# A decoder trunk with three branches on one core: rotary score products in pairs of pages, two products on 128 rows, and a table load, a low part and bank waits behind the prompt's heads

## The chip, the core and the metric

One Trainium2 chip, one of its cores. The metric is the device time of one execution in microseconds; three runs of the kernel before gave a median of 1589.9 us (1588.88 to 1589.93).

## What is computed

One inference step of a decoder trunk of two layers, for a prompt of 256 tokens and for 8 sequences of 8 new tokens each with 2048 cached positions (16 pages of 128). What matters here is the attention of the new tokens over the cached pages and over themselves, the causal attention of the prompt, and the spatial-gating branch:

```python
def attend(q_nope, q_pe, k_nope, k_pe, v, mask):
    s = (jnp.einsum('...qhd,...khd->...hqk', q_nope, k_nope)
         + jnp.einsum('...qhr,...kr->...hqk', q_pe, k_pe)).astype(jnp.float32) * ATTN_SCALE
    p = jax.nn.softmax(jnp.where(mask, s, NEG_INF), axis=-1).astype(v.dtype)
    return jnp.einsum('...hqk,...khd->...qhd', p, v)
# mla_sample, for one sequence: the latents of 16 pages and of the new tokens
k_nope, v = expand_kv(lat, w_ukv, k_nope_norm)   # k_nope is normalised per head
return attend(qn, qp, k_nope, kp, v, mask)
# sgu_branch: v in chunks of 128 tokens, w lower triangular
s = jnp.einsum('gts,bcsgd->bctgd', w, vp) + jnp.swapaxes(b_s, 0, 1)[:, :, None]
return u * s, v
```

## The kernel before

Everything is computed for 320 columns (T): 256 prompt tokens and 64 new ones. Each operand of a large product is split into a high part of type fp32r and the rest, a low part, and a product is run three times (high by high, high by low, low by high). The weights come as a stream of units of 128x1024, which ACT (w_hi) and DVE (w_lo) split. The program of each engine is written out by hand, in the order in which it runs, and semaphores tie the engines; nothing is moved by a scheduler. The eight banks of PSUM are handed on by semaphores bank_free, which the engine that reads a bank increments in `release(b)`.

A layer runs `project`, `spatial_and_attention_inputs`, `prompt_attention`, `pages`, `pages_end_and_first_round`, `second_round` and `ffn`, one function of each name per engine.

`prompt_attention` runs eight heads. For a head PE computes scores (`scores`, L984 to L988), DVE takes their maximum (`masked_max`, L1963 to L1966), ACT the exponentials (`exps`), DVE normalises (`normalised`, L1974 to L1977), PE transposes (L1014), ACT copies to pT, and PE multiplies by the values (`values`, L997 and L998) into the banks PAIR_BANK = (4, 6, 7, 5), one for two heads, which ACT (`pair_hi`) and DVE (`pair_lo`) empty. In the middle of the heads PE transposes v to tokens (`v_transposed`, L967) and multiplies by the spatial weights (`spatial`, L976 for 128 rows, L978 for the 64 new tokens), ACT and DVE compute the gate of that branch, y2, and split it. DVE also takes the low part of the spread rotary queries q128 (`rotary_spread_lo`, L1934). At head 6 ACT loads its logarithm and exponential table (`log_and_exp_tables`, L1318).

`pages` runs the 8 sequences, 16 pages each. Two of them are written out, then one more, then a hardware loop over pairs, then the last. The pages are loaded by SP in chunks of two, 4 chunks deep (tpage), with the latent transposed (256 columns) and the rotary key in 128 more: its 32 rows stand there four times, two times as high part and two times as low part, against the high and low parts of the query. ACT takes the high part of a chunk (`pages_hi`), DVE the low part of the latent (`pages_lo`, L1745) and POOL the low half of the rotary rows (`rotary_lo`, L711). For a page PE runs in `keys` one rotary product of 64 columns into bank 4, 5 or 6 and then twelve products of 288 columns into two banks, of which 256 are keys and 32 absorbed scores:

```python
r0 = HT * (p % (NPG // 2))
mm(PS[:, rotary_bank(p, par), r0:r0 + HT], lt_hi[:, t, i, 256:384], q128_of(b), start=True, stop=True)
```

ACT squares the keys (ksqp) and copies the scores (sraw), DVE sums the squares per head (kss, L2097). A sequence later its scores are finished: DVE multiplies them by the norms and adds the rotary scores from PSUM (`finished_scores`, at pages 4 and 5), takes the maximum over pages (`halves_max`, `page_max` L2051), PE transposes it (`seq_max`, L1058), DVE takes the row maximum, and PE spreads it over all rows with a product of 64 rows (`seq_spread`, L1063), DVE subtracts (`shift`), and ACT takes the exponential. Two sequences later the values of the pages are added (`page_values`, L1081 and L1082, at most two products a page), with rows loaded by SP (rrow), split by ACT (r_hi) and POOL (r_lo, L739). Before `pages` PE waits for seven banks and for q128; DVE splits y2 into y2_lo and copies snew before sequence 0, and POOL, before it goes on in sequence 0, waits for y2_lo and copies ones into r_hi (L753), since that lies over what y2_lo is computed from.

## Time and profile before

| | |
|---|---|
| median of 3 runs | 1589.9 us |
| profiled execution, its own time | 1589.27 us |
| its span in the trace | 1587.4 us |
| granted clock of TensorE | full in all slices |
| stages of pages | about 140 to 393 us and 927 to 1181 us |

The profile is of one execution. Its span runs from the first to the last instruction; the execution's own time has 1.9 us around it. Engines: PE is TensorE's products, PEld its weight loads, DVE VectorE, ACT ScalarE, POOL GpSimd, SP the queue that issues transfers. A PE row's duration holds the latency of its pipeline, so the rate of PE is read from one start to the next. The two layers run alike; times are quoted from the first.

### The profile page before, as it was taken

To read this page: it belongs to the slowest core of one execution; us is meant where nothing else is said; L and a number is where in the kernel's file an instruction comes from. 1 tells how busy PE (TensorE), PEld (TensorE's weight loads), DVE (VectorE), ACT (ScalarE), POOL (GpSimd) and SP (SyncE) were. 2 spreads that over 40 slices of the span, in tenths; PEclk is the share of its full clock that TensorE was granted. 3 is DMA by queue.
4 is the path that set the end of the run, shared out by engine and by line. 5 is a ranking of instruction groups with operands and counts; after the bars stand their busy time and mean duration, and the time that the engine had idled before them with its cause. 6 is when DMAs were issued, how large, how long until landed. Compare 5 with 4: busy or idle time off the path is not lost.

```text
span 1587.4 us, 33215 instructions
## 1 busy us (share of the span) xinstructions
PE 1561.0 (98%) x10860; PEld 1516.9 (96%) x10860; DVE 1068.7 (67%) x1626; ACT 884.6 (56%) x1612; POOL 521.1 (33%) x659
## 2 busy tenths in 40 slices
PE   7999999999999999999999999999999999999999
PEld 7987999999999999999999789999999999999999
DVE  6787777777664766664376877777775748666633
ACT  5786676767534444443357866666764345444432
POOL 3732377776700000000058213767667001000000
PEclk9999999999999999999999999999999999999999
DMA  7331455553544444444454224655535444444443
GB/s 274 120 108 52 139 183 167 163 161 109 186 134 155 151 147 146 150 155 146 146 188 136 76 73 137 196 152 166 163 111 174 145 154 151 147 146 146 151 152 112
DMA packets 114690, 232.90 MB, mean 147 GB/s; under 512 B 12881, under 2 KB 78706, under 8 KB 114450
## 3 DMA queue, kind: packets, MB, share of 16 engines
q1 hardware_dynamic: 112178, 223.13, 45.3%
q0 software_dynamic: 2400, 8.36, 1.6%
q8 instruction: 60, 0.98, 0.3%
q14 instruction: 52, 0.43, 0.1%
HBM read 228.98 MB, written 2.46 MB: 146 GB/s over the span
## 4 chain that ended last, share of the span: by engine, by line
PE 90%; DVE 4%; ACT 2%; DVEq 1%; issue 1%; ACTq 1%; DMA 0%; POOL 0%; SPq 0%; POOLq 0%
PE PS L803 53%; PE PS L1048 26%; PE PS L1081 2%; PE PS L1082 2%; DVE w_lo L1742 1%; PE PS L1043 1%; ACT w_hi L1297 1%; DVEq L1736 1%; PE PS L830 1%; PE PS L859 1%; ACTq L1301 0%; ACT r_hi L1297 0%; PE PS L937 0%; ACTq L1485 0%; DMA x<-in_xT 0%
## 5 line engine op out<-in xcount | busy, mean ns | idle before, releaser
L1742 DVE TENSOR_TENSOR w_lo<-raw,w_hi 128x1024 fp32r<-128x1024 f32 x258 | 325.0, 1261 | 222.9 <-ACT w_hi L1297 220.0
L1297 ACT ACTIVATE w_hi<-raw 128x1024 fp32r<-128x1024 f32 x258 | 272.3, 1057 | 347.3 <-PE PS L803 333.1
L803 PE MATMUL PS<-h_hi,w_hi 128*128 128x320 f32 x1360 | 426.4, 314 | 11.1 <-DVE h_lo L1769 10.3
L803 PE MATMUL PS<-h_hi,w_lo 128*128 128x320 f32 x1360 | 421.3, 310 | 0.0
L803 PE MATMUL PS<-h_lo,w_hi 128*128 128x320 f32 x1360 | 421.3, 310 | 0.0
L803 PEld LDWEIGHTS PS<-h_hi,w_hi 128*128 128x128 f32 x1360 | 256.3, 188 | 14.2 <-issue 9.5
L803 PEld LDWEIGHTS PS<-h_lo,w_hi 128*128 128x128 f32 x1360 | 256.4, 189 | 0.9
L803 PEld LDWEIGHTS PS<-h_hi,w_lo 128*128 128x128 f32 x1360 | 256.2, 188 | 0.0
L1048 PE MATMUL PS<-comb_hi,lt_hi 128*128 128x288 f32 x1024 | 239.9, 315 | 0.0
L1297 ACT ACTIVATE ksqp<-PS 128x512 f32<-128x512 f32 x256 | 153.2, 598 | 152.4 <-PE PS L1048 150.3
L2097 DVE TENSOR_REDUCE kss<-ksqp 128x8 f32<-128x512 f32 x256 | 174.2, 682 | 85.3 <-ACT ksqp L1297 84.2
L1048 PE MATMUL PS<-comb_hi,lt_lo 128*128 128x288 f32 x1024 | 218.7, 295 | 0.0
L1048 PE MATMUL PS<-comb_lo,lt_hi 128*128 128x288 f32 x1024 | 218.6, 294 | 0.0
L739 POOL TENSOR_TENSOR r_lo<-rrow,r_hi 128x512 fp32r<-128x512 f32 x128 | 167.7, 1314 | 42.1 <-issue 23.0
L711 POOL TENSOR_TENSOR lt_hi<-tpage,lt_hi 64x256 fp32r<-64x256 f32 x128 | 118.5, 925 | 169.7 <-ACT lt_hi L1297 165.3
L1048 PEld LDWEIGHTS PS<-comb_lo,lt_hi 128*128 128x128 f32 x1024 | 164.0, 188 | 0.0
L1048 PEld LDWEIGHTS PS<-comb_hi,lt_lo 128*128 128x128 f32 x1024 | 163.9, 188 | 0.0
L1048 PEld LDWEIGHTS PS<-comb_hi,lt_hi 128*128 128x128 f32 x1024 | 158.9, 189 | 0.0
L1745 DVE TENSOR_TENSOR lt_lo<-tpage,lt_hi 128x512 fp32r<-128x512 f32 x128 | 109.5, 856 | 26.9 <-ACT lt_hi L1297 26.6
L803 PE MATMUL PS<-hid_hi,w_lo 128*128 (+1 forms) x352 | 108.8, 309 | 0.0
L803 PE MATMUL PS<-hid_lo,w_hi 128*128 (+1 forms) x352 | 108.8, 309 | 0.0
L803 PE MATMUL PS<-hid_hi,w_hi 128*128 (+1 forms) x352 | 108.8, 309 | 0.0
(317 smaller groups left out, 2662.0 us busy)
## 6 DMA issues: line engine op xcount, KB each, us to landing
raw<-in_stream SPq DMA_DIRECT2D x258, 512.0 KB, 3.5
tpage<-in_tcache SPq DMA_DIRECT2D x256, 192.0 KB, 2.4
rrow<-in_rcache SPq DMA_DIRECT2D x256, 128.0 KB, 2.6
x<-in_xT SPq DMA_DIRECT2D x2, 640.0 KB, 6.9
sbias<-in_sbias POOLq DMA_DIRECT2D x2, 640.0 KB, 6.2
out_yT<-x SPq DMA_DIRECT2D x4, 320.0 KB, 2.2
const<-in_consts SPq DMA_DIRECT2D x1, 1088.0 KB
wgate<-in_wgate POOLq DMA_DIRECT2D x2, 512.0 KB, 4.5
```

The costliest lines, as they stand in the source:

```text
L711: nc.gpsimd.tensor_tensor(half, tpage[64:128, c % TBUF, :, 256:384], f(half), ALU.subtract).then_inc(pt_rope.sem, 1)
L739: nc.gpsimd.tensor_tensor(r_lo[:, at, :], rrow[:, src, :], f(r_hi[:, at, 0:KVL]), ALU.subtract).then_inc(rows_split.sem, 1)
L803: done = mm(out, w[:, slot, c], a, start=first and n == 0 and m == 0, stop=last and n == len(pairs) - 1 and m == 2)
L830: last = mm(out, lhsT, r, start=n == 0, stop=n == len(rhss) - 1)
L859: mm(PS[:, b, 0:T], wgate[:, g, j, :], xc[:, j, :], start=True, stop=True).then_inc(lgate_mm.sem, 1)
L1048: last = mm(PS[:, 2 * s + g, c0:c0 + 288], a[:, t, i, 128 * k:128 * k + 128], w[:, k, g, c0:c0 + 288], start=k == 0 and n == 0, stop=k == ...
L1081: mm(PS[:, 7, 0:KVL], w, r_lo[:, r, :], start=False, stop=False)
L1082: last = mm(PS[:, 7, 0:ROW], w, r_hi[:, r, :], start=False, stop=p == NPG - 1)
L1297: return nc.scalar.activation(out, in_, func, **kw)
L1742: V.tensor_tensor(w_lo[:, s, :], raw[:, s, :], f(w_hi[:, s, :]), ALU.subtract).then_inc(lo_done.sem, 1)
L1745: return V.tensor_tensor(out, whole, f(hi_), ALU.subtract)
L2097: V.tensor_reduce(kss[:, par, p, :], ksqp[:, s, :].rearrange("p (h c) -> p h c", h=H), AX.X, ALU.add).then_inc(pk_ss.sem, 1)
```

## The change

Four things are changed.

**Rotary scores.** The cache's rotary keys are laid out in blocks of 64 positions: the two halves of a page stand one above the other in 64 rows, high and low part make 128, and a chunk has 2 x 64 columns of them. PE runs one product of 256 columns for a chunk, in its second page: q_rot holds the high and the low part of the query, each for both halves with zeros between. The two results lie 128 elements apart in bank 6 or 5, and DVE adds them into srot with one reduction a chunk. POOL writes q_rot in `queries`. The key products keep their shapes, but take the same half of the two pages of a chunk together, and rrow is loaded in the same order. `finished_scores` adds srot instead of reading PSUM, and the waits on s_rot go away.

**128 rows.** `seq_spread` multiplies all 128 rows of mx, of which POOL zeroes the lower 64 once a layer. The new tokens' v is transposed together with 64 prompt tokens, and wss has 128 rows with zeros.

**Order in the heads.** ACT copies v_tokens before it squares ua. DVE has no rotary_spread_lo. ACT's table load moves from head 6 to page 10 of sequence 0.

**Behind the heads.** DVE's y2_lo moves to page 2, its copy of snew to page 6 of sequence 0. PE waits for banks 0 to 3 before sequence 0, for banks 6 and 5 at their first rotary products, and for 4 and 7 after the sequence.

```diff
@@ load_tpages, load_rows
-                sp.dma_start(rrow[:, (2 * m + i) % RRAW, :],
-                             ins["rcache"][bass.ds(l * NPHYS + at[i], 1)].rearrange("o p n -> p (o n)")
+                sp.dma_start(rrow[64 * i:64 * i + 64, 2 * m % RRAW:2 * m % RRAW + 2, :],
+                             ins["rcache"][bass.ds(l * NPHYS + at[i], 1)].rearrange("o (v r) n -> (o r) v n", v=2)
@@ POOL, queries
+                nc.gpsimd.tensor_tensor(hi_, both, half, ALU.mult)
                 pool.drain()
...
+                nc.gpsimd.tensor_tensor(lo_, both, f(hi_), ALU.subtract)
+                pool.drain()
+                nc.gpsimd.tensor_tensor(lo_, f(lo_), half, ALU.mult).then_inc(qc.sem, 1)
@@ POOL, sequence
                         for i in range(RROWS):
                             nc.gpsimd.tensor_copy(r_hi[:, i, KVL:ROW], ones[:, 0:2])
+                        pool.drain()
+                        nc.gpsimd.memset(mx[HT:128], 0.0)
                         pool.drain().then_inc(p_free.sem, 1)
@@ PE
-                mm(PS[:, 4 + g, SEQ:T], v_tokens[0:TS, 2, 128 * g:128 * g + 128], wss[:, g, :], start=True, stop=True).then_inc(sgu_mm.sem, 1)
+                mm(PS[:, 4 + g, SEQ:T], v_tokens[:, 2, 128 * g:128 * g + 128], wss[:, g, :], start=True, stop=True).then_inc(sgu_mm.sem, 1)
...
+        def rotary_scores(l, b, c, par):
+
+            pe.wait_ge(pt_rope.sem, pt_rope.at(l, b * NCH + (c + 1)))
+            if isinstance(b, int) and b == 0 and c < 2:
+                pe.wait_ge(bank_free[6 - c].sem, banks.last(l, 6 - c))
+            else:
+                pe.wait_ge(rot_added.sem, rot_added.at(l, b * NCH + (c - 1)))
+            mm(PS[:, 6 - c % 2, 0:4 * HT], lt_hi[:, c % 2, 4], q_rot[:, par].rearrange("p s c -> p (s c)"),
+               start=True, stop=True)
...
-            if p == NPG // 2 and not (isinstance(b, int) and b == 0):
-                pe.wait_ge(s_rot.sem, s_rot.at(l, b * 2))
-            r0 = HT * (p % (NPG // 2))
-            mm(PS[:, rotary_bank(p, par), r0:r0 + HT], lt_hi[:, t, i, 256:384], q128_of(b), start=True, stop=True)
+            if i == 1:
+                rotary_scores(l, b, p // CHUNK, par)
...
-            mm(PS[:, 4 + par, 128:128 + HT], ones[0:HT, :], mx[:, 1:1 + HT], start=True, stop=True).then_inc(s_mb.sem, 1)
+            mm(PS[:, bank, 128:128 + HT], ones[:], mx[:, 1:1 + HT], start=True, stop=True).then_inc(s_mb.sem, 1)
...
-            for b in (0, 1, 2, 3, 4, 6, 7):
+            for b in range(4):
+                pe.wait_ge(bank_free[b].sem, banks.last(l, b))
+            sequence(l, 0, 0, tail=False, values=False, older=False)
+            for b in (4, 7):
@@ ACT
             exps(0)
-            A(ge[:], ua[:], ACT.Square).then_inc(gsq.sem, 1)
             v_copied(l, 0, 4)
             v_copied(l, 1, 5)
             v_copied(l, 2, 7)
+            A(ge[:], ua[:], ACT.Square).then_inc(gsq.sem, 1)
...
-                if h == 6:
-                    log_and_exp_tables()
...
+                if not tail and p == 10:
+                    log_and_exp_tables()
@@ DVE
-            rotary_spread_lo(l, 0)
-            rotary_spread_lo(l, 1)
-            release(6)
...
+        def rotary_scores(l, b, c, par):
+
+            V.tensor_reduce(srot[:, par, 2 * c:2 * c + 2].rearrange("p v c -> p (v c)"),
+                            PS[:, 6 - c % 2, 0:4 * HT].rearrange("p (s x) -> p x s", s=2), AX.X, ALU.add).then_inc(rot_added.sem, 1)
...
+                if not tail and p == 2:
+                    dve.wait_ge(y2h.sem, y2h.at(l, 1))
+                    lo(y2_lo[:], ge[:], y2_hi[:]).then_inc(y2_ready.sem, 1)
+                if not tail and p == 6:
+                    dve.wait_ge(sn_ready.sem, sn_ready.at(l, 1))
+                    V.tensor_copy(snew[TS:2 * TS], snew[0:TS]).then_inc(sn_ready.sem, 1)
```

On PE, at the start of the stage of pages, there stood before (comb and lt are the key products' operands, q the spread query):

```order
L997 MATMUL PS<-pT,vp 64x256
L998 MATMUL PS<-pT,vp 64x128
L1043 MATMUL PS<-q,lt_hi 128x64
L1048 MATMUL PS<-comb_hi,lt_hi 128x288 x2
L1048 MATMUL PS<-comb_lo,lt_hi 128x288 x2
L1048 MATMUL PS<-comb_hi,lt_lo 128x288 x2
```

and the same place of the change, with the numbers at the rows' start since its rows read alike (the keys' rows of page 0 are 572 to 577, those of page 1 follow row 578):

```order
571 L1011 MATMUL PS<-pT,vp 64x128
572 L1064 MATMUL PS<-comb_hi,lt_hi 128x288 x2
573 L1064 MATMUL PS<-comb_lo,lt_hi 128x288 x2
574 L1064 MATMUL PS<-comb_hi,lt_lo 128x288 x2
575 L1064 MATMUL PS<-comb_hi,lt_hi 128x288 x2
576 L1064 MATMUL PS<-comb_lo,lt_hi 128x288 x2
577 L1064 MATMUL PS<-comb_hi,lt_lo 128x288 x2
578 L1043 MATMUL PS<-q_rot,lt_hi 128x256
```

The rotary product stands ahead of every second page now, and has 256 columns.

On DVE, at the same place, before (y_lo from PS is a pair of heads, y_lo from ge is y2_lo):

```order
L1745 TENSOR_TENSOR y_lo<-PS,y_hi 128x256 x3
L1745 TENSOR_TENSOR lt_lo<-tpage,lt_hi 128x512
L1745 TENSOR_TENSOR y_lo<-ge,y_hi 128x1280
L2017 COPY snew<-snew 64x512
L2097 TENSOR_REDUCE kss<-ksqp 128x8 x2
```

and in the change:

```order
L1757 TENSOR_TENSOR lt_lo<-tpage,lt_hi 128x512
L1757 TENSOR_TENSOR y_lo<-PS,y_hi 128x256 x2
L2098 TENSOR_REDUCE kss<-ksqp 128x8 x2
L2040 TENSOR_REDUCE srot<-PS 128x128
L1757 TENSOR_TENSOR lt_lo<-tpage,lt_hi 128x512
L2098 TENSOR_REDUCE kss<-ksqp 128x8
L1757 TENSOR_TENSOR y_lo<-ge,y_hi 128x1280
```

y2_lo has moved behind the sums of three pages, and the first reduction of rotary scores stands among them.

On POOL, around the start of sequence 0, the change has (lt_hi is the low half of the rotary rows):

```order
L722 TENSOR_TENSOR lt_hi<-tpage,lt_hi 64x128 x2
L764 CAST r_hi<-ones 128x2 x4
L766 MEMSET mx 64x67
L722 TENSOR_TENSOR lt_hi<-tpage,lt_hi 64x128 x14
```

The four copies, which wait for y2_lo, stand between the low halves of chunks 1 and 2, as before; the zeroing is new, and the low halves have 64x128 for 64x256.

## Rows read from the trace of the kernel before

**Rows 1.** The page's table of engines: busy us, share of the span, instructions

```profile
PE 1561.0 (98%) x10860; PEld 1516.9 (96%) x10860; DVE 1068.7 (67%) x1626; ACT 884.6 (56%) x1612; POOL 521.1 (33%) x659
```

**Rows 2.** Timeline of PE, sequence 0: start us, us, engine, line, operation

```profile
142.26 0.19 PE L1043 MATMUL PS<-q,lt_hi 128*128 128x64 f32 x1
...
142.64 0.42 PE L1048 MATMUL PS<-comb_lo,lt_hi 128*128 128x288 f32 x2
142.90 0.43 PE L1048 MATMUL PS<-comb_hi,lt_lo 128*128 128x288 f32 x2
...
143.96 0.19 PE L1043 MATMUL PS<-q,lt_hi 128*128 128x64 f32 x1
```

**Rows 3.** DVE in one sequence of the loop: stretch, us, busy, clock, DMA

```profile
259.68:292.34 32.66, 24.84 (x42) 1.00 0.54 163
```

**Rows 4.** Timeline of PE, a sequence of the loop, pages 13 to 14

```profile
322.54 0.28 PE L1081 MATMUL PS<-r_lo,p_hl 128*128 128x256 f32 x1
322.65 0.28 PE L1082 MATMUL PS<-r_hi,p_hl 128*128 128x258 f32 x1
...
322.86 0.43 PE L1063 MATMUL PS<-mx,ones 64*128 64x64 f32 x2
...
323.23 0.30 PE L1043 MATMUL PS<-q,lt_hi 128*128 x1
```

**Rows 5.** Timeline of PE, transposes of va and spatial products

```profile
111.93 1.47 PE L967 MATMUL PS<-const,va 128*128 128x128 f32 x12
...
116.23 0.71 PE L976 MATMUL PS<-wsp,v_tokens 128*128 128x128 f32 x4
116.88 0.43 PE L978 MATMUL PS<-wss,v_tokens 64*128 64x64 f32 x2
117.24 0.71 PE L976 MATMUL PS<-wsp,v_tokens 128*128 128x128 f32 x4
```

**Rows 6.** Timeline of all engines, heads to first page: [idle before <-releaser]

```profile
123.84 0.29 DVE L1963 TENSOR_REDUCE pst<-PS 128x1 f32<-128x128 f32 x1 [1.04 <-PE PS L988]
...
136.17 1.28 ACT L1318 ACT_TABLE_LOAD   x1 [0.16 <-issue]
...
136.91 0.55 PE L1014 MATMUL PS<-const,sp_ 128*128 128x128 f32 x3 [1.23 <-DVE sp_ L1977]
...
138.89 0.65 PE L997 MATMUL PS<-pT,vp 128*64 128x256 f32 x2
...
140.60 0.51 PE L1048 MATMUL PS<-comb_hi,lt_hi 128*128 128x288 f32 x2
```

**Rows 7.** Groups by line and shape: busy us, mean ns, idle before

```profile
L1297 ACT ACTIVATE ksqp<-PS 128x512 f32<-128x512 f32 x256 | 153.2, 598 | 152.4 <-PE PS L1048 150.3
L2097 DVE TENSOR_REDUCE kss<-ksqp 128x8 f32<-128x512 f32 x256 | 174.2, 682 | 85.3 <-ACT ksqp L1297 84.2
...
L2051 DVE TENSOR_REDUCE m<-mxh 128x64 f32<-128x512 f32 x16 | 17.3, 1084 | 1.4
...
L1964 DVE TENSOR_REDUCE pst<-PS 128x1 f32<-128x256 f32 x16 | 6.6, 413 | 0.0
```

**Rows 8.** Line L1745: duration ns min/median/max, first and last start

```profile
L1745 DVE TENSOR_TENSOR y_lo<-ti,y_hi x2: 1483/1483/1483, 106.8 to 893.9; 128x1280 fp32r<-128x1280 f32 x2
```

**Rows 9.** Timeline of POOL, sequence 0

```profile
143.75 0.70 POOL L753 CAST r_hi<-ones 128x2 fp32r<-128x2 f32 x4 [1.52 <-DVE y_lo L1745]
145.85 1.07 POOL L711 TENSOR_TENSOR lt_hi<-tpage,lt_hi 64x256 fp32r<-64x256 f32 x1 [1.41 <-ACT lt_hi L1297]
```

**Rows 10.** Groups by line and shape, POOL

```profile
L698 POOL TENSOR_TENSOR comb_lo<-qabs,comb_hi 128x64 fp32r<-128x64 f32 x32 | 9.9, 330 | 2.4 <-issue 0.8
```

**Rows 11.** Timelines of PE and DVE, sequence 1, pages 7 and 8

```profile
179.62 0.20 PE L1043 MATMUL PS<-q,lt_hi 128*128 128x64 f32 x1
...
180.97 0.68 DVE L1745 TENSOR_TENSOR lt_lo<-tpage,lt_hi 128x512 fp32r<-128x512 f32 x1
...
181.71 0.30 PE L1043 MATMUL PS<-q,lt_hi 128*128 128x64 f32 x1 [0.23 <-DVE lt_lo L1745]
```

More of the change, by code:

```diff
@@ L1926, in spatial_and_attention_inputs @@
             lo(y0_lo[:], ti[:], y0_hi[:]).then_inc(y0_ready.sem, 1)
-        def rotary_spread_lo(l, jt):
-            dve.wait_ge(q128_hi.sem, q128_hi.at(l, 1))
-            for r in (1, 3):
-                rows = slice(32 * r, 32 * r + 32)
-                dst = q128[rows, :, 32 * jt:32 * jt + 32].rearrange("p b (h t) -> p h b t", h=4)
-                src = PS[rows, 6, :].rearrange("p (h j b t) -> p h j b t", h=4, j=2, b=NB)[:, :, jt]
-                last = V.tensor_tensor(dst, src, f(dst), ALU.subtract)
-            last.then_inc(q128_ready.sem, 1)
         def new_latent_lo(l):
@@ L2010, in prompt_attention @@
             normalised(7)
-            for j in range(1, 4):
-                pair_lo(l, j)
+            pair_lo(l, 1)
             pages_lo(l, 0, 1)
-            dve.wait_ge(y2h.sem, y2h.at(l, 1))
-            lo(y2_lo[:], ge[:], y2_hi[:]).then_inc(y2_ready.sem, 1)
-            dve.wait_ge(sn_ready.sem, sn_ready.at(l, 1))
-            V.tensor_copy(snew[TS:2 * TS], snew[0:TS]).then_inc(sn_ready.sem, 1)
+            pair_lo(l, 2)
+            pair_lo(l, 3)
         def pair_lo(l, j):
@@ L2032, in finished_scores @@
             half = NPG // 2
-            at, bank = (slice(half, NPG), 6) if second else (slice(0, half), 4 + par)
+            at = slice(half, NPG) if second else slice(0, half)
             inv = kss[:, par, at].rearrange("p a (h o) -> p a h o", o=1).to_broadcast([128, half, H, NT])
@@ L2037, in finished_scores @@
             dve.drain()
-            into = sraw[:, par, at].rearrange("p a c -> p (a c)")
-            last = V.tensor_tensor(into, into, PS[:, bank, :], ALU.add)
-            last.then_inc(s_rot.sem, 1)
+            V.tensor_tensor(sraw[:, par, at], sraw[:, par, at], srot[:, par, at], ALU.add)
+        def rotary_scores(l, b, c, par):
+            V.tensor_reduce(srot[:, par, 2 * c:2 * c + 2].rearrange("p v c -> p (v c)"),
+                            PS[:, 6 - c % 2, 0:4 * HT].rearrange("p (s x) -> p x s", s=2), AX.X, ALU.add).then_inc(rot_added.sem, 1)
         def of_seq(t, b):
```

131 lines of the change are left out of this document (67 added, 64 removed).

## Prediction

> **What bounds the kernel now.** I read the page's table of engines first, then the timeline of TensorE over the cache pages, then the rows of the engine that TensorE waits for at each place where its rhythm breaks. The table shows PE busy 98% of the span and DVE 67% [rows 1]: almost everything that shortens the time must shorten PE's own row, or one of its few waits. The clock was granted in full throughout. In sequence 0 a page is one rotary product and twelve key products, and pages start every 1.70 us (142.26 to 143.96, [rows 2]). Where I say page 8 or page 12 I mean the place in a sequence of 16 pages. The loop over the later sequences is the same rhythm with two value products more per page. DVE is busy 24.8 of 32.7 us in a sequence of the loop [rows 3], so 8 us are free there, but in pieces.
>
> **The rotary products.** A pair of key products starts every 0.265 us (12 products are 1.59 us), so of the 1.70 us the one 64-column rotary product costs 0.106 us [rows 2]. The change runs one product of 256 columns per two pages instead of two of 64. The nearest row is a value product with 256 columns, after which the next starts 0.11 us later [rows 4]; I take 0.12. A chunk of two pages saves 2 x 0.106 - 0.12 = 0.09 us, 64 chunks a layer: **5.9 us a layer**. The bounds are narrow, 5.5 to 6.5.
>
> **The spread of the maximum.** It has 64 rows now. From the last value product (322.65 + 0.12) to the next page at 323.23 pass 0.46 us for two passes of 64 columns [rows 4]. With 128 rows the nearest price is the transposes of va, 12 in 1.47 us with their tail, 0.12 each [rows 5]: two are 0.24. Saving 0.22 x 8 = **1.8 us a layer** (bounds 0 and 2.7). The zeroing of mx is one small POOL instruction a layer.
>
> **The new tokens' spatial products.** A group of four passes with 128 rows takes 0.65 us (116.23 to 116.88), and the two with 64 rows 0.36 (to 117.24) [rows 5]. At 0.12 each the six would take 0.72 instead of 1.01: 1.2 us over four groups. Besides, the square of ua is behind the three copies of v_tokens now, so that PE need not wait for the third. The third transpose has 128 columns for 64: under 0.2 us. DVE loses four subtractions (rotary_spread_lo). PE comes out about 1.5 us sooner, and the heads can use it, since DVE stood 1.04 us for PE's scores in the middle of them [rows 6]. I take **1.5 us a layer**, between 0.4 (ACT's row is then the bound) and 2.4.
>
> **The table load and the bank waits.** The load of 1.28 us at 136.17 stands on ACT between the last head's exponentials and the next copy of pT. The last head's transposes end at 136.91 + 0.55 = 137.46; a copy of 0.5 and a semaphore later its value product could start at 138.1; it starts at 138.89. From there PE needs some 0.7 us (the product's row is 0.65), and the first page could start at 138.8. It starts at 140.60, because it waits for seven banks, whose last is released by DVE [rows 6]. Now it waits for banks 0 to 3 only: **1.8 us a layer** (bounds 0.8 and 2.0). In its new place, page 10 of sequence 0, the load lies in ACT's idle time; if that cover were gone it would cost its 1.28 us.
>
> **What is late next: y2's low part.** This is the one new wait that I price against the change. DVE splits y2 after page 2 of sequence 0 now. POOL waits for it before it copies ones into r_hi, and behind that wait stands POOL's low half for chunk 2, for which PE's rotary product in page 5 waits. Counted from the first key product: pages 0 to 2 end at 3 x 1.59 + 0.12 = 4.9; ACT's square 0.60 and DVE's reduction 0.68 with two semaphores make 6.3 [rows 7]; the split takes 1.48 with POOL idle [rows 8]: 7.8. POOL then takes 0.17 and 0.70 for the four copies, some 0.3 for the zeroing and two drains, 0.25 to its next instruction and some 0.45 for it (64x128 now, between the 0.33 of a 128x64 and the 1.07 of a 64x256) [rows 9, 10]: 9.7 to 9.9. PE reaches the product at 5 x 1.59 + 2 x 0.12 = 8.2. **PE stands some 1.6 us a layer** (0 to 2.5). The start of y2's high part and SP's loads of rows come later too, but nothing needs them before sequence 2.
>
> **The reductions on DVE.** DVE gets one reduction a chunk: 256 PSUM elements, summed in pairs 128 elements apart. The trace has no such read. Its bounds are the 256 contiguous PSUM elements at 413 ns, and the per-element rate of the strided SBUF row. The contiguous rows of 512 and 256 elements (682 and 413 ns) give 1.05 ns an element and 144 ns a start; the strided one has (1084 - 144)/512 = 1.84 ns, which for 256 and a start gives 0.62 us [rows 7]. I take 0.50, 0.45 in the row of a busy engine. Eight are 3.6 us a sequence, so DVE comes to 28.5 of 32. Where DVE is slack that is hidden. It is not at page 8: in sequence 1 PE's page 8 starts 2.09 us after page 7 instead of 1.71, at 181.71, and the wait ends with DVE's lt_lo, started 180.97 [rows 11]. The reduction of page 5 lies on that chain, and PE's three pages before it are 0.15 shorter: it costs 0.6 there. A second place is page 12, behind page_max: 0.4 more by the same reckoning. That gives back 1.0 us in sequence 1. In the loop the same chain has 3 x 0.24 us more room, so of the 0.38 + 0.6 some 0.3 are left a sequence, six times 1.8. **Together 2.8 us a layer** (0 to 5).
>
> The Trainium skill says on its page Vector Engine (DVE) Microarchitecture Reference, section Measured stream behaviour on trn2, that an SBUF port keeps its rate only for runs of at least two adjacent words, and that a source hopping every element takes 1.73 instead of 1.05 ns. By that rule the reduction would take about 0.59 us (an estimate from that page) and the sum would come out some 2 us higher. The strided row of this trace (1.84 ns) agrees with it for SBUF in kind; that page gives no figure for PSUM, and no row here has one.
>
> **Other parts.** ACT's high copy of pages has 640 for 768 elements, and POOL's low half is half as long, both off the path. POOL's queries get three 128x128 operations a sequence, some 1.4 us, against the eight shorter halves. The last add of scores reads SBUF for PSUM. They cost nothing while POOL keeps a microsecond of lead into the next sequence; if not, the first pages wait some tenths.
>
> **Sum.** A layer saves 5.9 + 1.8 + 1.5 + 1.8 = 11.0 and gives back 1.6 + 2.8 = 4.4: 6.6, for two layers 13 us. The profiled execution took 1589.27 us beside a span of 1587.4, and becomes 1576.3; the median of the three runs lies 0.6 above it: **1577 us** (0.8% faster; its own range 1572 to 1582).
>
> **Rivals.**
> Nothing is given back: y2's split comes early enough or POOL catches up, and DVE's idle pieces take the reductions. For it: DVE has 8 us free a sequence. Against it: the wait at page 8 is there already. 2 x 11.0 off: 1568.
> DVE is the bound in places: the reduction takes its upper bound, and heads gain only 0.7 because ACT's row sets their pace. Then 1.5 us a layer more go in the stages of pages and 0.8 in the heads, and POOL's longer queries hold up some first pages: 1583.
> The gain at the heads is only a deferral: DVE enters sequence 0 later by the y2 split and the copy of snew, and all that PE won is spent in waits there, while the loop is held by DVE at today's pace. 1588 to 1590.
> Slower: DVE becomes the bound everywhere. It decides from (32 - 25)/8 = 0.85 us a reduction; if pairs from PSUM cost what the whole strided row costs now, 1.08 us [rows 7], DVE needs 24.8 + 8.6 + 0.6 = 34.0 us a sequence instead of 32.7, some 9 us a layer over seven sequences, against which the heads and sequence 0 save 2.4 in all: 6.6 a layer, 1603. For it speaks only that PSUM's price is unseen; against it that the row has twice the elements.
>
> **Chances.** Forecast 0.48, nothing given back 0.17, DVE in places 0.18, deferral 0.10, slower 0.07. A measurement of this kernel can tell 0.2% (3.2 us) from no change. The first three are faster (0.83), the deferral is no change (0.10), the last slower (0.07). The range has to take in 1568 and 1583 with an edge for unknown prices: 1566 to 1587.
>
> **What would show it.** PE's pages in the middle of sequence 0 should start 1.59 and 1.71 us apart by turns; the 256-column rotary product should cost its successor 0.12 us. A wait of PE at page 5 of sequence 0 should end with POOL's low half, about 1.6 us long. The first key product should come 3.3 us sooner after the layer's start. The reduction's duration decides most of the rest: at 0.41 the loop's sequence should be 31.6 us, at 0.62 over 32.2. If the first key product comes no sooner, the heads' terms are wrong; if the loop's sequences stay at 32.7, those of the rotary products are.

## The result, and the profile after

The changed kernel takes **1595.33 us** (median of 6 runs, 1594.70 to 1596.18) where the kernel before, on the same chip, takes 1589.91 (6 runs, 1588.88 to 1590.93): 5.4 us longer, ratio 1.0035 with the interval [1.0022, 1.0048]. The forecast was 1577, its range 1566 to 1587. The profiled execution took 1595.93 us beside a span of 1594.1.

The page's table of engines, after (answers to [rows 1]):

```profile
span 1594.1 us, 33203 instructions
PE 1547.3 (97%) x10732; PEld 1502.8 (94%) x10732; DVE 1117.2 (70%) x1746; ACT 870.6 (55%) x1612; POOL 519.6 (33%) x709
```

PE has 13.7 us less to do and DVE 48.5 more. So PE does not work longer, it waits longer. What it waits for, in the waits of PE after (what it waited for, us in total, times, longest):

```profile
PE PS L1064 <- DVE lt_lo L1757: 18.3, 24, 1.7
PE PS L1094 <- POOL r_lo L750: 4.0, 10, 1.2
PE PS L1043 <- ACT sraw L1309: 2.8, 2, 1.4
```

The first row is new in its size: before, a page began with its rotary product, and those products waited 0.4 us in all for lt_lo. The third is the wait at page 5 of sequence 0. The gain and the loss by stage, from the timelines of PE, for layer 1 and layer 2 (a layer's heads are counted from the first product with wv_first to the first key product, a sequence from its first key product to that of the next):

| stage | before | after | difference |
|---|---|---|---|
| heads | 38.8, 38.4 | 36.5, 36.2 | -2.3, -2.2 |
| sequence 0 | 27.1, 27.1 | 28.0, 28.0 | +0.9, +0.9 |
| sequence 1 | 28.7, 28.7 | 28.8, 28.8 | 0.0, 0.0 |
| sequence 2 to the last value product | 244.0, 244.9 | 248.7, 248.6 | +4.7, +3.7 |
| ahead of layer 1's heads, and from layer 1's last value product to layer 2's heads | 101.9, 448.5 | 101.1, 450.1 | -0.8, +1.6 |

The differences sum to the 6.7 us between the spans. The last line holds nothing that the change touches; its parts differed by 1 to 2 us between other profiles of this study too, and its +1.6 is a matter of TensorE's clock: from 804.9 to 808.2 us of the profile after it was granted at half (1.2 for 2.4 GHz), behind three waits of PE of 0.4 us each; the profile before has it in full there. The loss lies in the loop: a sequence there takes 33.8 to 34.1 us (in layer 2 every second one 32.9) against some 32.8 before [rows 3]. The rest of the two profiles is told where the stall is.

PE at page 8 of a loop sequence, after (start, length, engine, line, what; in brackets the idle time before it and its releaser): it stands for 1.73 us.

```profile
276.05 0.28 PE L1095 MATMUL PS<-r_hi,p_hl 128*128 128x258 f32 x1
278.06 0.53 PE L1064 MATMUL PS<-comb_hi,lt_hi 128*128 128x288 f32 x2 [1.73 <-DVE lt_lo L1757]
```

What DVE did up to there, and POOL beside it, after (same columns):

```profile
270.85 0.69 DVE L2098 TENSOR_REDUCE kss<-ksqp 128x8 f32<-128x512 f32 x1 [0.22 <-ACT ksqp L1309]
271.45 0.95 DVE L2034 TENSOR_TENSOR sraw<-sraw,kss 128x512 f32<-128x512 f32 x1
272.48 1.53 DVE L2036 TENSOR_TENSOR sraw<-sraw,srot 128x512 f32<-128x512 f32 x1
273.92 0.67 DVE L2098 TENSOR_REDUCE kss<-ksqp 128x8 f32<-128x512 f32 x1
274.52 0.41 DVE L2040 TENSOR_REDUCE srot<-PS 128x128 f32<-128x256 f32 x1
274.85 0.67 DVE L2034 TENSOR_TENSOR sraw<-sraw,kss 128x512 f32<-128x512 f32 x1
275.60 1.52 DVE L2036 TENSOR_TENSOR sraw<-sraw,srot 128x512 f32<-128x512 f32 x1
277.05 0.88 DVE L1757 TENSOR_TENSOR lt_lo<-tpage,lt_hi 128x512 fp32r<-128x512 f32 x1
...
272.17 1.29 POOL L750 TENSOR_TENSOR r_lo<-rrow,r_hi 128x512 fp32r<-128x512 f32 x1 [0.32 <-issue]
...
275.04 1.53 POOL L750 TENSOR_TENSOR r_lo<-rrow,r_hi 128x512 fp32r<-128x512 f32 x1 [0.32 <-issue]
```

The same piece of the kernel before, DVE and then POOL, in rows that the prediction did not read:

```profile
272.30 0.69 DVE L2097 TENSOR_REDUCE kss<-ksqp 128x8 f32<-128x512 f32 x1 [0.47 <-ACT ksqp L1297]
272.90 0.96 DVE L2036 TENSOR_TENSOR sraw<-sraw,kss 128x512 f32<-128x512 f32 x1
273.94 0.69 DVE L2039 TENSOR_TENSOR sraw<-sraw,PS 128x512 f32<-128x512 f32 x1
...
275.90 0.69 DVE L2039 TENSOR_TENSOR sraw<-sraw,PS 128x512 f32<-128x512 f32 x1
276.50 0.68 DVE L1745 TENSOR_TENSOR lt_lo<-tpage,lt_hi 128x512 fp32r<-128x512 f32 x1
...
273.63 1.29 POOL L739 TENSOR_TENSOR r_lo<-rrow,r_hi 128x512 fp32r<-128x512 f32 x1 [0.32 <-issue]
```

From the start of the reduction of page 4 to the end of lt_lo DVE took 4.88 us before (272.30 to 277.18) and 7.08 after (270.85 to 277.93). The 2.20 us more are the two adds (2 x 0.83 = 1.67), the new reduction (0.33, to the start of the next instruction) and lt_lo (0.20). The add is as large as before; what has changed is that its second operand is srot in SBUF where it was PSUM, and that it runs beside a subtraction of POOL with two SBUF operands. Beside the same POOL instruction the add from PSUM took 0.69.

Not every add of the change is stretched. In the two sequences of layer 2's loop that take 32.9 us both adds take 0.8, and POOL's subtraction starts 0.6 us after them where it starts 0.3 to 0.6 before them elsewhere; page 8 then starts 2.4 us after page 7, for 3.7 in the other sequences of the loop. So one execution of one kernel shows both cases, 1.0 us a sequence apart. In all, 14 of the 32 adds took 1.5 us.

The groups of DVE over a loop sequence (stretch 258 to 292, count, busy us, mean ns), after:

```profile
L2040 DVE TENSOR_REDUCE srot<-PS 128x128 f32<-128x256 f32 x9 | 3.7, 412 | 0.0
L2036 DVE TENSOR_TENSOR sraw<-sraw,srot 128x512 f32<-128x512 f32 x2 | 3.0, 1524 | 0.1
```

The reduction takes 0.41, the lower of its two bounds (0.41 and 0.62, taken at 0.50). The row that the prediction valued at nothing, the add, is the dear one.

From here on, **theory A**: page 8 waits for the two halves of the finished scores that stand in a row on DVE, and these grew by the stretched adds. **Theory B**: DVE is short of time as a whole, from 128 reductions.

### The profile page after: what moved, and what is told of

The parts are those of the page before. It is cut to its first block, busy times and chain, and to the rows that moved or that the text cites. A ratio compares the mean times of both kernels' runs of the same rounds, so it can differ in the third digit from the quotient of the medians.

```text
span 1594.1 us, 33203 instructions
## 1 busy us (share of the span) xinstructions
PE 1547.3 (97%) x10732; PEld 1502.8 (94%) x10732; DVE 1117.2 (70%) x1746; ACT 870.6 (55%) x1612; POOL 519.6 (33%) x709
## 4 chain that ended last, share of the span: by engine, by line
PE 76%; DVE 11%; DVEq 4%; ACT 3%; issue 3%; ACTq 1%; DMA 1%; SPq 0%; POOL 0%; POOLq 0%
PE PS L816 53%; PE PS L1064 17%; DVEq L2035 2%; DVE lt_lo L1757 2%; DVE kss L2098 2%; DVE w_lo L1754 1%; PE PS L1094 1%; ACT ksqp L1309 1%; PE PS L1095 1%; DVEq L1748 1%; ACT w_hi L1309 1%; DVE m L2052 1%; DVE srot L2040 1%; DVE sraw L2036 1%; PE PS L1043 1%
## 5 line engine op out<-in xcount | busy, mean ns | idle before, releaser
L1064 PE MATMUL PS<-comb_hi,lt_hi 128*128 128x288 f32 x1024 | 224.4, 300 | 19.1 <-DVE lt_lo L1757 18.3
L2098 DVE TENSOR_REDUCE kss<-ksqp 128x8 f32<-128x512 f32 x256 | 170.9, 679 | 61.1 <-ACT ksqp L1309 60.2
L722 POOL TENSOR_TENSOR lt_hi<-tpage,lt_hi 64x128 fp32r<-64x128 f32 x128 | 80.3, 628 | 165.9 <-ACT lt_hi L1309 157.4
```

The lines of the kernel that those rows point to most:

```text
L722: nc.gpsimd.tensor_tensor(half, tpage[64:128, c % TBUF, :, 4], f(half), ALU.subtract).then_inc(pt_rope.sem, 1)
L1064: last = mm(PS[:, 2 * s + g, c0:c0 + 288], a[:, t, 2 * k + i], w[:, k, g, c0:c0 + 288], start=k == 0 and n == 0, stop=k == 1 and n == 2)
L2098: V.tensor_reduce(kss[:, par, p, :], ksqp[:, s, :].rearrange("p (h c) -> p h c", h=H), AX.X, ALU.add).then_inc(pk_ss.sem, 1)
```

## The experiments

Each was timed beside the kernel before; the ratio is to that, and it is what compares kernels of different rounds best. Line numbers of rows are those of the kernel that the rows are from; edits are to the changed kernel where nothing else is said.

**1. Without the add.**

```diff
-            dve.drain()
-            V.tensor_tensor(sraw[:, par, at], sraw[:, par, at], srot[:, par, at], ALU.add)
```

> The add of the rotary scores to the key scores is left out (two instructions of 512 elements a sequence on DVE, line 2036), with its drain. The output leaves the rotary part of the sample scores out. THEORY A, the chain to page 8: the wait of PE for DVE's low half at page 8 is ended by the two halves of finished scores that stand in a row on DVE at pages 4 and 5; the adds take 1.52 us each there, where before they took 0.69. Without them the chain is 3.0 us shorter, the loop's sequence falls from 33.9 to 31.9 or 32.2 us, and the kernel takes 1570 to 1578. THEORY B, sheer load: DVE is filled by the 128 reductions; the add is 3 of its 29.4 us a sequence, and the time falls by no more than the load is above some limit: 1585 or more.

Measured: 1578.40 us, ratio 0.9932 [0.9918, 0.9945]: 17 us less than the changed kernel for 32 instructions of 1.11 us on average. The loop's sequences take 32.1 to 32.9 us. PE's wait for lt_lo is down to 5.2 us from 18.3:

```profile
PE PS L1064 <- DVE lt_lo L1757: 5.2, 13, 0.5
```

Just above A's range, and far from B's. But it takes the whole add away, its old 0.69 us too.

**2. Short reductions.**

```diff
-            V.tensor_reduce(srot[:, par, 2 * c:2 * c + 2]...,
+            n = 2 * HT if isinstance(b, int) and b < 2 else 8
+            V.tensor_reduce(srot[:, par, 2 * c:2 * c + 2]...[:, 0:n],
```

> From sequence 2 on the reduction over two products sums 8 of 128 columns, so that it takes some 0.16 us for 0.41; the order and every wait stay. The output leaves out most of the rotary part there. THEORY A (chain to page 8): of the eight reductions a sequence only the one of page 5 (and that of page 7, for pages later) lies on the chain, so a loop's sequence of 33.9 us gains 0.25 to 0.6, and the kernel takes 1588 to 1593. THEORY B (sheer load of the reductions): 2.0 us less DVE work in each of six sequences of two layers gives most of it back, 1.5 or more a sequence: 1577 or less.

Measured: 1594.07 us, ratio 1.0027 [1.0018, 1.0036], 1.3 us less than the changed kernel, which the two intervals do not tell apart from nothing. Page 8 starts 3.45 us after page 7 instead of 3.70: the saving of the one reduction of page 5, and hardly anything for the seven others. In layer 2 all the loop's adds are stretched now, and the two sequences that took 32.9 us take 33.5, which uses up part of the gain. B falls. A's range (1588 to 1593) was missed by a microsecond.

**3. The pieces apart.**

```diff
-                if tail and p in (4, 5):
-                    finished_scores(l, b - 1, 1 - par, p == 5)
+                if tail and p in (4, 6):
+                    finished_scores(l, b - 1, 1 - par, p == 6)
-                if tail and p == 7:
+                if tail and p == 8:
                     halves_max(l, b - 1, 1 - par)
-                if tail and p == 9:
+                if tail and p == 10:
                     page_max(l, b - 1, 1 - par)
```

> Same work, same instructions: the second half of the finished scores stands after page 6 instead of page 5, halves_max after 8 instead of 7, page_max after 10 instead of 9, so that the low half of the next pages stands between the two long pieces. THEORY A (chain to page 8): no piece between two low halves is longer than 2.5 us, PE's waits at pages 8 and 12 mostly go, the loop's sequence falls from 33.9 to 32.0 to 32.6 and the kernel takes 1572 to 1582. THEORY B (sheer load): DVE has the same 29.4 us a sequence to do; the kernel takes 1593 to 1597.

Measured: 1591.95 us, ratio 1.0012 [1.0003, 1.0021], a miss for A's number and for B's. The wait at page 8 is gone in every sequence (1.6 to 1.8 us for up to 3.7), but PE now stands in page 11, before the transpose of the maxima (L1071), for up to 1.7 us, since page_max comes after it is wanted:

```profile
PE PS L1071 <- issue: 10.2, 8, 1.5
PE PS L1071 <- DVE m L2054: 8.7, 6, 1.7
```

The same profile has the add in both conditions, within one sequence. The first starts while POOL's r_lo runs, the second while a copy of POOL (L734) does. DVE, then POOL:

```profile
272.78 1.53 DVE L2036 TENSOR_TENSOR sraw<-sraw,srot 128x512 f32<-128x512 f32 x1
...
277.51 0.73 DVE L2036 TENSOR_TENSOR sraw<-sraw,srot 128x512 f32<-128x512 f32 x1
...
272.47 1.28 POOL L750 TENSOR_TENSOR r_lo<-rrow,r_hi 128x512 fp32r<-128x512 f32 x1 [0.32 <-issue]
...
276.83 0.86 POOL L734 CAST p_hl<-prob 128x256 fp32r<-128x256 f32 x1
277.83 1.01 POOL L736 TENSOR_TENSOR p_hl<-prob,p_hl 128x256 fp32r<-128x256 f32 x1
```

The add takes 0.73 us where POOL's copy has only 0.18 us left to run, and 1.53 where r_lo has 0.97 left (272.78 to 273.75). Both adds end 0.55 us after the POOL instruction that was running when they started (273.75 to 274.31, 277.69 to 278.24), as if the add waited for its end. That holds for every such add of this study: in each of the nine profiles with all adds from SBUF, 26 of the 32 started beside a running POOL instruction, and all of them end 0.54 or 0.55 us after it; those that started alone take 0.69.

**4. The change without its rotary products.** From the kernel before: table load at page 10, the square behind the copies, 128-row products, y2's low part after page 2, bank waits behind the heads.

> The kernel before, with every part of the change but the paired rotary products: table load at page 10, the square of ua behind the copies, spatial and spread products on 128 rows, y2's low part after page 2, bank waits behind the heads. The low part of q_rot stays with DVE in the heads. THEORY A: the head's gain (2.1 to 2.3 us a layer) and the spread's (0.22 x 8) are real and y2's low part costs 1.6 us at page 4 or 5 of sequence 0: 2.4 us a layer less than before, 1583 to 1587. RIVAL, deferral: what the head gains is waited for in sequence 0, and the spread's gain is lost to DVE's chain: 1589 to 1591.

Measured: 1592.56 us, ratio 1.0017 [1.0008, 1.0026], slower than before and outside both ranges. The heads save 2.3 and 1.7 us and the spread 0.32 a sequence (page 14 after 2.17 us for 2.49), but sequence 0 takes 33.7 us (32.6 in layer 2) for 27.1: its rotary product stands in page 4, a page sooner than the paired one, and needs POOL's low half of chunk 2 there:

```profile
141.61 0.19 PE L1048 MATMUL PS<-q,lt_hi 128*128 128x64 f32 x1
147.19 0.39 PE L1048 MATMUL PS<-q,lt_hi 128*128 128x64 f32 x1 [3.73 <-issue]
150.43 0.26 PE L1048 MATMUL PS<-q,lt_hi 128*128 128x64 f32 x1
```

Page 5 starts 3.1 us after it, for 1.7, and that is the clock: during the stand of 3.73 us it fell, and it was granted at half up to 152.4. By the starts of the pages behind the stand that cost 2.4 us in layer 1 and 1.4 in layer 2. A stretch of page 4 (us, busy of PE, PEld, DVE, ACT and POOL, then the granted clock, 0.50, and DMA):

```profile
147.20:150.30 3.10, 3.10 (x13) 3.10 (x14) 0.00 (x0) 0.00 (x0) 0.72 (x1) 0.50 0.42 128
```

With the old rotary products y2's move is dearer.

**5. An add from PSUM, first try.**

```diff
+                    pe.wait_ge(pt_lo.sem, pt_lo.at(l, b * NCH + 5))
                     seq_sums(l, b - 3, 4)
...
-            V.tensor_tensor(sraw[:, par, at], sraw[:, par, at], srot[:, par, at], ALU.add)
+            V.tensor_tensor(into, into, PS[:, 4, :], ALU.add)
```

> The changed kernel with one operand replaced: the two adds of a sequence read 512 columns of PSUM (bank 4) where they read srot in SBUF; the reductions stay, and so does all else (PE waits at page 6 for the low half of chunk 4 before the sums, which it does at page 8 anyway). The sample scores have no rotary part. THEORY A (both DVE and POOL fetch two SBUF operands, and slow each other): the add is back at 0.69 us in the loop from 1.52, page 8 stalls 1.6 us less, a loop's sequence takes 32.2 to 32.8 us for 33.9 and the kernel 1579 to 1586, close to the kernel without the add plus 2 x 0.69 us where DVE has no room. THEORY B (the add is long for its own sake, or the load of the reductions is the cause): the add stays over 1.1 us or the sequence over 33.4, and the kernel at 1592 or more.

Measured: 1622.48 us, ratio 1.0200 [1.0186, 1.0214]. The experiment is spoiled by its own wait, which I took for one that PE has anyway; at page 6 it comes two pages early, and behind the long waits the granted clock fell, to 0.987 to 0.992 on average in its runs:

```profile
PE PS L1101 <- DVE lt_lo L1758: 28.2, 10, 3.0
```

What it shows is the duration alone: 0.69 us for every add of the loop.

**6. As 4, with POOL's wait for y2 later.**

```diff
-                    if c == 0 and isinstance(b, int) and b == 0:
+                    if c == 4 and isinstance(b, int) and b == 0:
                         pool.wait_ge(y2_ready.sem, y2_ready.at(l, 1))
```

> As the kernel with the old rotary products and the rest of the change, but POOL's wait for y2's low part (with its four copies of ones and the zeroing) stands after chunk 4 of sequence 0 and not before the low half of chunk 2. THEORY A (that wait is what sequence 0 pays, 5.4 us a layer with a rotary product in page 4): sequence 0 is back at 26.9 us and the kernel takes 1580 to 1584, 6 to 10 less than before. RIVAL (PE's gain in the heads is waited for anyway, since DVE's chain of sums behind y2_lo is what holds page 4): 1589 to 1593.

Measured: 1581.33 us, ratio 0.9941 [0.9927, 0.9954]. Sequence 0 is back at 27.2 us in both layers. POOL's wait, in front of a low half that PE needs at once, is what sequence 0 paid: 11.9 us in the two layers, of which some 4 are the clock behind it.

**7. Finished scores after 4 and 6 only**, halves_max and page_max left at 7 and 9, and the edit of 6.

> The changed kernel with the finished scores after pages 4 and 6 (for 4 and 5), halves_max and page_max where they were (7 and 9), and POOL's wait for y2 after chunk 4 of sequence 0. THEORY A: sequence 0 loses its 1.7 us stall; page 8 does not stall, PE waits at pages 10 to 12 for some 0.5 us; loop's sequence 32.0 to 32.6; kernel 1576 to 1583. THEORY B (any place of these pieces gives the same, since DVE is short of time as a whole): 1588 to 1592, only the stall of sequence 0 gone.

Measured: 1581.53 us, ratio 0.9942 [0.9929, 0.9956], in A's range. Page 8 has no wait; most loop sequences have one at page 10, again for lt_lo (page 10 starts 3.7 us after page 9, for 2.2), and last 33.0 to 33.4 us (two of layer 2's without it 32.2 and 32.6).

**8. Everything behind page_max a page later** (finished scores after 4 and 6, halves_max 8, page_max 10, transpose and row maximum 12, spread and shift 14, exponentials 15), and the edit of 6.

> Finished scores after 4 and 6, halves_max after 8, page_max after 10, and what follows it one page later each: PE's transpose of the maxima at page 12 and its spread at 14, DVE's row maximum at 12 and shift at 14, ACT's exponentials at 15; POOL's wait for y2 after chunk 4 of sequence 0. THEORY A: the 1.7 us that PE stood before the transpose at page 11 are covered too; loop's sequence 31.2 to 32.0; kernel 1569 to 1577. RIVAL: the exponentials come a page later, and POOL's split and PE's first value product at page 3 of the next sequence wait for them: 0.5 to 1.5 us a sequence, 1578 to 1588. THEORY B (DVE is short of time as a whole): 1588 to 1592.

Measured: 1588.04 us, ratio 0.9982 [0.9973, 0.9991]: the upper end of the rival's range, and the lower end of B's. The trace decides between them: no wait is left at pages 8 to 13, but page 0 starts 2.4 to 2.6 us after page 15, for 1.8, and the end of the stage, where the last two sequences have only value products, waits for POOL's r_lo, which comes after the exponentials. At those last waits the granted clock fell to half, for 6.8 us in each layer, which makes up to 7 us in this profile.

```profile
PE PS L1094 <- POOL r_lo L750: 10.1, 12, 3.7
```

**9. The order that fits.** Finished scores after 4 and 6, halves_max after 8, page_max after 10, the transpose of the maxima after 12, and the rest where it was; the row maximum goes ahead of page 12's reduction; and the edit of 6. It computes all that the reference does.

```diff
-                if tail and p == 11:
+                if tail and p == 12:
                     seq_max(l, b - 1, 4)
...
+                if tail and p == 12:
+                    row_max(l, b - 1, 4)
                 dve.wait_ge(pk_sq.sem, pk_sq.at(l, b * NPG + (p + 1)))
```

> The changed kernel with finished scores after pages 4 and 6, halves_max after 8, page_max after 10, PE's transpose of the maxima after page 12 (for 11), DVE's row maximum ahead of the reduction of page 12, and everything behind it (spread, shift, exponentials) where it was; POOL's wait for y2 after chunk 4 of sequence 0. THEORY A (page 8 and page 12 are single places where a piece of DVE work stands ahead of what PE needs): none of the stalls of the earlier orders is left, a loop's sequence takes 31.2 to 31.9 us, and the kernel 1560 to 1570. THEORY B (DVE's load, 29 us in 32, makes a stall come back at another page whatever the order): 32.3 or more a sequence, 1577 or more.

Measured: **1567.57 us** (1566.48 to 1569.70), ratio 0.9863 [0.9848, 0.9878]: 22.4 us under the kernel before, 27.8 under the changed one. The same instructions on DVE, the adds as stretched as in 7 (1130 ns on average in both loops, for 1340 in the changed kernel's: the order takes the second add away from r_lo too), the same reductions. Loop sequences take 31.5 to 32.2 us; one is the distance of these rows of PE (the first value product of a sequence):

```profile
260.65 0.28 PE L1090 MATMUL PS<-r_hi,p_hl 128*128 128x258 f32 x1
...
292.57 0.28 PE L1090 MATMUL PS<-r_hi,p_hl 128*128 128x258 f32 x1
```

The waits of PE have no lt_lo among their large ones any more; what the maxima still cost is this:

```profile
PE PS L1076 <- DVE mx L2060: 1.6, 6, 0.3
```

**10. The changed kernel with the edit of 6 alone.**

> The changed kernel with one edit: POOL's wait for y2's low part, its copies of ones and the zeroing stand after chunk 4 of sequence 0. If the stall in page 5 of sequence 0 comes from that wait, sequence 0 falls from 28.0 to 26.3 us, and the kernel from 1595.3 to 1591.5 to 1592.5. If DVE's split of y2 itself (kss of pages 3 and 4 stand behind it) holds page 5, the stall stays: 1594 to 1596.

Measured: 1591.93 us, ratio 1.0014 [1.0005, 1.0023]: 3.4 us less than the changed kernel, and 24.4 more than 9, which is what the order alone is worth. Its rotary products of sequence 0 start 3.28 us apart throughout, where the changed kernel's go like this:

```profile
139.23 0.28 PE L1043 MATMUL PS<-q_rot,lt_hi 128*128 128x256 f32 x1
142.51 0.28 PE L1043 MATMUL PS<-q_rot,lt_hi 128*128 128x256 f32 x1
147.37 0.36 PE L1043 MATMUL PS<-q_rot,lt_hi 128*128 128x256 f32 x1 [1.42 <-ACT sraw L1309]
```

4.86 for 3.28: 1.58 us lost. The profile names ACT, whose copy came last by its records; POOL's low half was the one that counted, since the edit touches only POOL.

**11. The table load back at head 6.**

> The changed kernel with the load of the table back at head 6. If the load stood between the last head's exponentials and the next copy of pT on the path, the first key product comes 0.6 to 1.3 us later after the layer's first product than in the changed kernel (36.5 us), and the kernel takes 1.2 to 2.6 us longer: 1596.5 to 1598. If the bank waits had hidden it: 1594.5 to 1596.

Measured: 1597.74 us, ratio 1.0044 [1.0030, 1.0057]: 2.4 us more than the changed kernel, with intervals that overlap. The first key product comes 38.0 and 37.1 us after the layer's first product with wv_first (36.5 and 36.2). In layer 1 part of that is the clock, at half from about 137 to 140 us in this profile; layer 2, without it, says 0.9 us for the load. And the wait of the kernel before is back:

```profile
PE PS L1010 <- ACT pT L1309: 1.3, 2, 0.6
```

**12. The order of 9 with the old rotary products.**

> The fastest order so far (finished scores after 4 and 6, halves_max after 8, page_max after 10, transpose of the maxima after 12, POOL's wait for y2 after chunk 4) with the rotary products of the kernel before: one of 64 columns a page, no reductions, adds from PSUM. If the paired products are worth what was forecast (0.09 us a chunk, 64 chunks a layer, 11.8 us in all) where DVE makes nobody wait, this kernel takes 11 to 13 us more than the paired one of the same order: 1578 to 1581. If DVE's reductions and adds still give part of it back there, the gap is smaller: 1570 to 1577.

Measured: 1592.13 us, ratio 1.0009 [1.0000, 1.0017], outside what I expected, and 10.8 us slower than 6, which has the old order. The rotary product of page 8 writes the bank from which the second add reads, and waits for that add, now a page later:

```profile
PE PS L1048 <- DVE sraw L2041: 6.1, 8, 1.3
```

(In six more sequences the profile names ACT's copy for the wait at this place, 3.6 us in all. In the one I read, that copy ended 0.16 us after the add; which of the two counted is not shown.)

So the paired kernel can be ordered in a way that the old one cannot: its rotary scores leave PSUM in two pages. For the worth of the paired products I compare each with the order that suits it: 1567.57 against 1581.33, 13.8 us by the medians, 12.4 by the ratios, 11.8 in the two profiles from the first key product to the last value product of both layers. What of this is PE's own row and what the order cannot be told from these two.

**13 and 14. An add from PSUM, with a control.** In both, the older sequence's sums and normalising stand after page 8 and its transposes and their copy after 10, so that PE touches bank 4 only behind a wait that it has; in 14 the adds read PSUM as in 5.

> A control for the next: the changed kernel with the older sequence's sums after page 8 (for 6), its normalising after 8 (for 7), its transposes after 10 and their copy after 10 (for 9). DVE gets the same work; the pieces in front of page 8 stay: 1594 to 1597, page 8 at 3.5 us or more in the loop.

> The same with the two adds of a sequence reading 512 columns of PSUM (bank 4) for srot in SBUF; PE touches that bank only from page 8 on, behind a wait that it has anyway. The sample scores have no rotary part. THEORY A (the stretch of an add with two SBUF operands beside POOL's is what page 8 waits for): the add takes 0.69 for 1.52 us, page 8 comes 1.6 us sooner and a loop's sequence 1.2 to 1.6: 10 to 16 us under the control. RIVAL (the reduction of page 5 and the adds' bare 0.69 are enough for the stall): under 5 us below the control.

Measured: the control 1613.78 us, ratio 1.0149 [1.0135, 1.0163], the other 1601.90, ratio 1.0072 [1.0060, 1.0084]. The control missed its range by 17 us: the copy of the transposes after page 10 holds up the transpose of the maxima at page 11, a wait that both have (13.4 and 13.2 us, 10 times). Between the two lie **11.9 us**, within A's 10 to 16, but not all by A's way: page 8 starts 3.1 us after page 7 instead of 3.9, 0.8 sooner where A said 1.6. Two things make up the 11.9. PE waits 7.5 us less for lt_lo:

```profile
PE PS L1064 <- DVE lt_lo L1757: 18.1, 16, 2.0
PE PS L1064 <- DVE lt_lo L1757: 10.6, 16, 1.1
```

(control, then the other). The rest is mostly the clock: after PE had stood 1.96 us at page 8, the control's clock was granted at half, and page 9 came 3.4 us after page 8 without a wait in it:

```profile
281.50:284.80 3.30, 3.30 (x17) 3.30 (x16) 3.21 (x5) 0.71 (x2) 1.38 (x2) 0.50 0.42 122
```

The control's runs have a mean granted clock of 0.995 to 0.997, the other's 0.999 to 1.000; 0.003 of 1614 us are some 5 us (an estimate). The changed kernel's profile has the clock in full through both stages of pages, so its own loss there holds nothing of the kind. Where the stretch went shows on DVE (then POOL) of the kernel with the PSUM operand:

```profile
272.43 0.69 DVE L2038 TENSOR_TENSOR sraw<-sraw,PS 128x512 f32<-128x512 f32 x1
...
275.32 1.70 DVE L1757 TENSOR_TENSOR lt_lo<-tpage,lt_hi 128x512 fp32r<-128x512 f32 x1
...
272.12 1.29 POOL L750 TENSOR_TENSOR r_lo<-rrow,r_hi 128x512 fp32r<-128x512 f32 x1 [0.32 <-issue]
...
275.28 1.19 POOL L750 TENSOR_TENSOR r_lo<-rrow,r_hi 128x512 fp32r<-128x512 f32 x1 [0.32 <-issue]
```

The add from PSUM is untouched by POOL's r_lo that started 0.31 us before it; lt_lo, with two SBUF operands, now meets the next one and takes 1.70. (lt_lo, too, ends 0.55 us after r_lo.) Some of what the add no longer pays, lt_lo pays, so that 7.5 us is the price of the stretch in this order, not of the operand in every one.

## Why the prediction was wrong

**The step that failed** stands under "Other parts": "The last add of scores reads SBUF for PSUM. They cost nothing". The add went from 0.69 to 1.53 us in 7 of the 16 sequences, two a sequence, and to 0.8 in five more. It stood on the chain to page 8, which the same prediction had named as the place where DVE has no room [rows 11]; the reduction was priced there and the add was not. Experiments 13 and 14 put its stretch at some 7.5 us of waiting, which agrees with the 1.0 us by which the stretched sequences of layer 2 are longer than the others, seven times; experiment 1 puts the whole add at 17.

How far that goes in the 18 us of the miss: by the prediction's terms, sequence 2 to the last value product should have saved 4.0 us a layer (six times the sum of 0.74 and 0.22, less 1.8), and lost 4.7 and 3.7. These 16 us are most of the miss, and the heads make 2 of the rest; sequences 0 and 1 came out as forecast. About half of the 16 is the stretch. The rest is what else grew on DVE's way to pages 8 and 12, so that the term "0.3 are left a sequence" was too small by more than the add alone: the reduction of page 5 (0.33 us) and lt_lo's own stretch (0.20) stand there, and with adds from PSUM PE still waited 10.6 us for lt_lo. How that rest divides is not shown.

**Two SBUF operands beside POOL.** The rows say that a DVE subtraction or addition with two SBUF operands takes 0.7 us alone and up to 1.7 beside POOL's. The Trainium skill, page SBUF — State Buffer, section Who interferes with whom, says that a DVE instruction with two SBUF inputs contends with a GpSimd instruction that reads SBUF, since its second input comes through the shared read interface. It calls the shared ports an exclusive lock; that whoever issues first has them for the whole instruction it says of DVE's two-port modes. The rows agree, with the whole-instruction part for these instructions too: every add that starts beside a running POOL instruction ends 0.55 us after it, 0.73 or 1.53 us long in experiment 3, and with the PSUM operand it takes 0.69 beside the same POOL row in experiment 14. The kernel before had the sign of it too: lt_lo took 0.68 at 276.50 and 1.23 at 280.32, ending 0.55 us after a subtraction of POOL (279.90 to 281.00).

**The sign of the result** was not in the rival that had it. "DVE becomes the bound everywhere" wanted a reduction of 0.85 us; it takes 0.41, and DVE was no bound: the order of experiment 9 has the same work and runs a sequence in 31.5 to 32.2 us. The stall was local.

**Rotary products: right.** Two pages and one rotary product take 3.28 us in sequence 0, for 3.39: 0.11 saved a chunk, against a forecast of 0.09. In the best order tried for each, the kernels with and without pairing are 12 to 14 us apart, against 11.8. The prediction's sign, that the rotary terms are wrong if the loop's sequences stay at 32.7, would have misled: the sequences grew, and the terms held.

**Spread of the maximum: right, undersized.** Forecast 0.22 us, 0.32 in experiment 4.

**Heads: two thirds.** Forecast 1.5 + 1.8 = 3.3 us a layer, measured 2.3 and 2.2. The table load and the bank waits gave their 1.8: from the last head's transposes to the first key product pass 1.92 us (135.62 to 137.54) for 3.69 [rows 6], and experiment 11 gives the load alone 0.9 of it. The groups of spatial products start 0.67 us apart for 1.00, as forecast, but of the 1.5 us only 0.5 arrived at the first page: PE now waits 1.08 us for DVE (at 120.03) before the first head's value product, where it had no wait before, and the last heads still wait 1.23 us for sp_. The lower bound of 0.4 was near, and its reason (another engine sets the heads' pace) the right one.

**y2's low part: right.** Forecast 1.6 us a layer, 1.58 in the timeline, 3.4 for both layers in experiment 10.

**Reductions: overpriced.** Taken at 0.50 us, with 2.8 us a layer given back. They take 0.41, and experiment 2, which cut them by some 0.25 us each in six sequences of eight, gave 1.3 us in all. The 0.59 us that the prediction worked out from the Trainium skill's figure for a source that hops every element did not come: the measurement decides for 0.41. Besides, the same section excepts a one-source instruction whose stream alternates between two regions and writes one word for two read, as this reduction does (there the regions lay 16 KiB apart, here 512 bytes, in PSUM). The wait at page 8 was named rightly, its cause only in part.

**The forecast gain itself** was there: experiment 9 takes 1567.57, where "nothing is given back" said 1568. That agreement is partly luck, since its order also removes waits of the kernel before (page 8 and 12 of sequence 1) while the heads gave less.

## What to carry to other kernels

When an edit moves an operand from PSUM to SBUF, price the instruction anew: look whether the other vector engine reads SBUF at the same time, and whether somebody waits behind it. A place that is named as having no room must be summed over all that stands there, moved and changed instructions as well as new ones. Before giving up a change that lost time, put its long pieces between the short ones that others wait for: here the order alone was worth 24 us, and each wait had to be followed to its next place (page 8, page 10, page 11, the stage's end) until one order had hardly any. And read the granted clock before you give a difference to one cause: in experiments 4, 5, 8, 11 and 13 it had fallen at a wait of PE, and part of the time was that.

## What was not expected of the hardware

A DVE add of 512 elements with both operands in SBUF took 0.69 us alone; started while an instruction of POOL ran, it ended 0.55 us after that instruction, however long that had still to run, and so took 0.73 behind the end of a copy and 1.53 behind a subtraction of 512 elements. From PSUM it took 0.69 beside the same subtraction. Small and one-source instructions stretch as well: over the whole execution the 64-element maximum (L2054) went from 0.27 to 0.53 us on average, and the scaling of olat (L2078), which has one tensor operand in SBUF, from 0.51 to 0.87. A reduction that pairs PSUM elements 128 apart ran at 412 ns for 256 elements, the same as contiguous ones [rows 7].
